# Value pages loaded straight from the cache, and no page copied while index queries run: a hybrid decoder step on one Trainium2 core

## The reference

```python
h = _rmsnorm(x, g_mix_pre)
q, k, v, iq, ik, iw, u = jnp.split(h @ w_in, IN_OFFSETS, axis=-1)
# sample rows: index scores over the paged indexer keys, then attention over the kept keys
ik_past = cache_kidx_l[page_table]
s = relu(einsum('bqhd,bsd->bqsh', iq, ik_all) * IDX_DIM**-0.5)
scores = einsum('bqsh,bqh->bqs', s, iw * N_IDX_HEADS**-0.5)
idx = top_k(scores, 256)
k_sel = cache_k_l[phys, slot]; v_sel = cache_v_l[phys, slot]
a = softmax(q @ k_sel * HEAD_DIM**-0.5) @ v_sel
p = pooling mixer of u (windows 2, 4, 8, 16)
x = x + _rmsnorm([a ; p] @ w_o, g_mix_post)
x = x + _rmsnorm(conv_gated_ffn(_rmsnorm(x, g_ffn_pre)), g_ffn_post)
```

## Time and profile before

| | |
|---|---|
| median of 3 runs | 1183.36 us |
| the profiled execution | 1183.83 us |
| its span, first to last instruction | 1182.0 us |
| mean granted clock | 0.994 |
| PE busy | 1155.7 us, 98% |
| DVE busy | 806.9 us, 68% |
| ACT busy | 531.5 us, 45% |
| POOL busy | 55.3 us, 5% |
| DMA moved | 238.76 MB, mean 202 GB/s |

### The profile page before, as it was taken

The page is one execution under the profiler, slowest core; times in us unless marked ns, Lnnn a source line. Parts: engine busy times, 40 slices in busy tenths (PEclk is TensorE's granted clock), DMA queues, the critical chain, the costliest instruction groups (busy, mean ns, idle before and its releaser), DMA issues.

```text
span 1182.0 us, 25876 instructions
## 1 busy us (share of the span) xinstructions
PE 1155.7 (98%) x9172; PEld 1119.0 (95%) x9172; DVE 806.9 (68%) x1523; ACT 531.5 (45%) x753; POOL 55.3 (5%) x66
## 2 busy tenths in 40 slices
PE   8989999999998999999999999999999999999998
PEld 7879999867897899999999999999999999999997
DVE  4775798876478877777777777777777544444443
ACT  7342333434245655454545454545455433333332
POOL 4710000000003100000000000000000000000000
PEclk9999999999999999999999999999999999999999
DMA  8977878768852565545555555555556866666651
GB/s 310 317 262 246 257 244 304 256 211 274 306 202 91 184 206 164 189 164 188 167 185 169 184 171 181 171 183 170 183 168 185 264 178 179 180 180 185 181 166 74
DMA packets 81080, 238.76 MB, mean 202 GB/s; under 512 B 9440, under 2 KB 28992, under 8 KB 78704
## 3 DMA queue, kind: packets, MB, share of 16 engines
q1 hardware_dynamic: 75152, 225.40, 59.5%
q10 hardware_dynamic: 4480, 9.01, 2.2%
q0 software_dynamic: 1408, 3.84, 1.0%
HBM read 231.64 MB, written 24.16 MB: 216 GB/s over the span
## 4 chain that ended last, share of the span: by engine, by line
PE 89%; DVE 4%; DMA 2%; SPq 2%; issue 1%; ACT 1%; POOL 0%; DVEq 0%; ACTq 0%; POOLq 0%
PE bank L1475 28%; PE bank L1476 28%; PE bank L1478 28%; DMA raw<-in_w_in 2%; DVE part L1344 1%; DMA cache_ring<-kscr 1%; DVE lo L443 1%; PE bank L1692 1%; SPq L486 1%; SPq L485 1%; DVE h_lo L1349 1%; PE bank L1668 0%; PE bank L1844 0%; SPq L484 0%; PE bank L1657 0%
## 5 line engine op out<-in xcount | busy, mean ns | idle before, releaser
L1475 PE MATMUL bank<-h_hi,hi 128*128 128x266 f32 (+1 forms) x2096 | 604.1, 288 | 1.5 <-DVE lo L443 1.5
L1478 PE MATMUL bank<-h_hi,lo 128*128 128x266 f32 (+1 forms) x2096 | 602.8, 288 | 0.0
L1476 PE MATMUL bank<-h_lo,hi 128*128 128x266 f32 (+1 forms) x2096 | 602.1, 287 | 0.0
L443 DVE TENSOR_TENSOR lo<-raw,hi 128x1024 fp32r<-128x1024 f32 (+2 forms) x362 | 431.6, 1198 | 208.1 <-ACT hi L435 194.5
L435 ACT ACTIVATE hi<-raw 128x1024 fp32r<-128x1024 f32 (+2 forms) x362 | 373.5, 1034 | 287.8 <-PE bank L1478 265.0
L1475 PEld LDWEIGHTS bank<-h_hi,hi 128*128 128x128 f32 x2096 | 397.4, 190 | 6.0 <-issue 3.9
L1476 PEld LDWEIGHTS bank<-h_lo,hi 128*128 128x128 f32 x2096 | 396.0, 189 | 0.1
L1478 PEld LDWEIGHTS bank<-h_hi,lo 128*128 128x128 f32 x2096 | 395.7, 189 | 0.0
L1476 PE MATMUL bank<-g_lo,hi 128*128 128x264 f32 x704 | 200.5, 285 | 0.0
L1478 PE MATMUL bank<-g_hi,lo 128*128 128x264 f32 x704 | 199.6, 284 | 0.0
L1475 PE MATMUL bank<-g_hi,hi 128*128 128x264 f32 x704 | 199.4, 283 | 0.0
(11 more groups left out here) (279 smaller groups left out, 612.6 us busy)
## 6 DMA issues: line engine op xcount, KB each, us to landing
raw<-in_w_up SPq DMA_DIRECT2D x176, 512.0 KB, 3.8
raw<-in_w_in SPq DMA_DIRECT2D x56, 512.0 KB, 5.0
raw<-in_w_down SPq DMA_DIRECT2D x64, 448.0 KB, 3.5
raw<-in_w_o SPq DMA_DIRECT2D x32, 512.0 KB, 4.8
raw<-in_w_down SPq DMA_DIRECT2D x32, 512.0 KB, 3.8
kscr<-in_cache_k SPq DMA_DIRECT2D x64, 128.0 KB
vscr<-in_cache_v SPq DMA_DIRECT2D x64, 128.0 KB
mixed<-kscr SPq DMA_DIRECT2D x8, 512.0 KB, 7.2
```

What stands on the lines that cost most here:

```text
L443: ops.tensor_tensor(lo[:, s, 0:width], raw[:, s, 0:width], hi[:, s, 0:width].bitcast(F32), ALU.subtract).then_inc(done, 1)
L1475: mm(out, w_hi, x_hi[:, k, first:], start=(opens and done == 0), stop=False)
L1476: mm(out, w_hi, x_lo[:, k, first:], start=False, stop=False)
L1478: last = mm(out, w_lo, x_hi[:, k, first:], start=False, stop=(closes and done == total))
```

## The change

- Value pages are no longer copied to `vscr`. `load_v` reads 8 page numbers and issues 8 DMAs of 128 KB from the cache straight into the slot; the waits for the slot stay as they were. POOL issues it for sequences 0, 1, 4 and 7, SP for 2, 3, 5 and 6.
- Key pages are still copied (`key_page`), but none while index queries load: SP issues the loads of index tiles 0 to 7 alone, then 4 key pages, then 3 behind each of the 20 projection tiles.
- POOL loads the causal mask only when the last part of x has landed, and begins the gathers of indexer keys once PE is through index tile 0.
- ACT rounds the first index-query chunk after all 16 blocks of h instead of after 13, and issues the loads of `pool_w` and `state_pool` after the sample index scores instead of before the index heads.

```diff
+        def load_v(eng, b):
+            if b < GROUPS:
+                eng.wait_ge(kq_used, 4)
...
+            for g in range(PAGES):
+                n = PAGES * b + g
+                page = eng.value_load(ptrow[0:1, n:n + 1], min_val=0, max_val=a["cache_v"].shape[0] - 1)
+                eng.dma_start(value_slot(b)[:, g, :], a["cache_v"][page]).then_inc(v_loaded[b], 16)
...
-                sp.dma_start(vscr[n], a["cache_v"][page]).then_inc(scr_loaded, 16)
...
+            for t in range(8):
+                load_in(0, C_IQ + 2 * t, t)
             sp.wait_ge(pt_loaded, 48)
...
+            for n in range(4):
+                key_page(n)
+            def paced_in(i, t, n0):
+                load_in(i, C_IQ + 2 * t, 2 * i + t)
+                for k in range(3):
+                    key_page(6 * i + n0 + k)
+            with sp.Fori(0, 10) as i:
+                paced_in(i, 8, 4)
+                paced_in(i, 9, 7)
...
                 if u in (5, 6):
-                    load_v(2 * u - 10)
-                    load_v(2 * u - 9)
-            load_v(4)
+                    load_v(sp, u - 3)
             load_wo(17)
-            load_v(5)
+            load_v(sp, 5)
             load_wo(18)
-            load_v(6)
-            load_v(7)
+            load_v(sp, 6)
...
+            pool.wait_ge(x_loaded[len(X_PARTS) - 2], 16)
             pool.dma_start(S[:, :], a["causal"]).then_inc(s_loaded, 16)
             pool.wait_ge(kix_ready, 1)
+            pool.wait_ge(chunk_used, C_IQ + 2)
...
+            for b in (0, 1, 4, 7):
+                load_v(pool, b)
...
-                if k == 13:
-                    hi_chunk(ae, 0, C_IQ)
                 nc.scalar.activation(h_hi[:, k, :], x0[:, k, :], ACT.Copy,
                                      scale=par[:, G1 + k:G1 + k + 1]).then_inc(h_hi_ready, 1)
+            hi_chunk(ae, 0, C_IQ)
             hi_chunk(ae, 0, C_IQ + 1)
...
-                    pe.wait_ge(v_loaded[GROUPS * r + j], 16)
+                    pe.wait_ge(v_loaded[GROUPS * r + j], 16 * PAGES)
```

More of the change, by code:

```diff
@@ L320, in build_program @@
     kscr = nc.dram_tensor("kscr", [DB * PAGES, P, KV * PAGE], F32).ap()
-    vscr = nc.dram_tensor("vscr", [DB * PAGES, P, KV * HD], F32).ap()
     xscr = nc.dram_tensor("xscr", [P, KM, TG], F32).ap()
@@ L463, in load_x @@
             eng.dma_start(x0[:, part_n, :], a["x"][:, part_n, :]).then_inc(x_loaded[n], 16)
+        def load_v(eng, b):
+            if b < GROUPS:
+                eng.wait_ge(kq_used, 4)
+            elif b == GROUPS:
+                eng.wait_ge(score_done, NU)
+            elif b == GROUPS + 1:
+                eng.wait_ge(pv_done, NU)
+            else:
+                eng.wait_ge(spv_done, 1)
+            for g in range(PAGES):
+                n = PAGES * b + g
+                page = eng.value_load(ptrow[0:1, n:n + 1], min_val=0, max_val=a["cache_v"].shape[0] - 1)
+                eng.dma_start(value_slot(b)[:, g, :], a["cache_v"][page]).then_inc(v_loaded[b], 16)
         @block.sync
@@ L480, in _, with key_page @@
                     load(0, C_IK + j, a["w_ik"][:, j * 8 * IKW:(j + 1) * 8 * IKW], 8 * IKW)
-            def pages(n):
+            def key_page(n):
                 page = sp.value_load(ptrow[0:1, bass.ds(n, 1)], min_val=0, max_val=a["cache_k"].shape[0] - 1)
                 sp.dma_start(kscr[n], a["cache_k"][page]).then_inc(scr_loaded, 16)
-                sp.dma_start(vscr[n], a["cache_v"][page]).then_inc(scr_loaded, 16)
             w_in = a["w_in"]
@@ L493, in load_in @@
                     load(r, cj + j, w_in[t, :, j * CW:(j + 1) * CW])
-            load_in(0, C_IQ, 0)
+            for t in range(8):
+                load_in(0, C_IQ + 2 * t, t)
             sp.wait_ge(pt_loaded, 48)
[L498 to L517, removed]
+            for n in range(4):
[7 more added lines that the diff above has]
+                paced_in(i, 9, 7)
+            k_src = kscr.rearrange("(b g) p e -> b p g e", b=DB)
             def load_k(r, c):
@@ L523, in load_k @@
                     b, pages_c = GROUPS * r + j, key_pages(c)
[L524 to L535, removed]
+                    sp.dma_start(page_slot(b)[:, pages_c], k_src[b][:, pages_c]).then_inc(k_loaded[j][c], 16)
             def load_wo(n):
@@ L543, in _ @@
                 load_wo(n)
-            sp.wait_ge(scr_loaded, 2 * DB * PAGES * 16)
+            sp.wait_ge(scr_loaded, DB * PAGES * 16)
             sp.wait_ge(sidx_done, 1)
@@ L679, in _ @@
             root(1)
-            ae.wait_ge(h_lo_ready, KM)
-            ae.dma_start(partf[:, 0:2048], a["pool_w"]).then_inc(poolw_loaded, 16)
-            ae.dma_start(partf[:, 2048:2048 + 960], a["state_pool"]).then_inc(poolw_loaded, 16)
             IDX_SCALE = float(IDX_DIM) ** -0.5 * float(IDX_HEADS) ** -0.5
@@ L724, in _ @@
                                  scale=IDX_SCALE).then_inc(srelu_done, 1)
+            ae.wait_ge(h_lo_ready, KM)
+            ae.dma_start(partf[:, 0:2048], a["pool_w"]).then_inc(poolw_loaded, 16)
+            ae.dma_start(partf[:, 2048:2048 + 960], a["state_pool"]).then_inc(poolw_loaded, 16)
             with ae.Fori(0, 7) as i:
```

## The result

| | before | after |
|---|---|---|
| median of the runs compared | 1184.24 us (6 runs) | 1190.46 us (6 runs, 1187.93 to 1191.10) |
| ratio after to before | | 1.0041, interval 1.0031 to 1.0051 |
| profiled execution, its span | 1183.83, 1182.0 us | 1190.06, 1188.3 us |
| mean granted clock | 0.994 | 0.990 |
| DMA moved | 238.76 MB | 230.37 MB |

The change made the kernel slower, by about 4.9 us (3.7 to 6.0) as the ratio has it; the forecast was 1186.1 us, 2.7 us above the median of the runs shown then. The two medians of the table lie 6.2 us apart, which is outside that interval; the text goes by the ratio on record. A second comparison (number 6) gave 1.0039 (1.0026 to 1.0052), with medians 4.7 us apart.

A forecast was written before the change was run, and what follows sets the result against it. PE, busy 1155.7 of 1182.0 us, was taken as the bound. From 1183.83 us: start -1.0, index stage -1.6, its clock -1.5, value pages +5.6, clock there +1.0 gave 1186.3, set at 1186.1 us; range 1180 to 1193.5.

The forecast's parts named there:

- second rival: At the value pages, POOL's page read is dear, 1.6 us or more: 1194.5 us; chance 0.13.
- Its own case: At the value pages, POOL decides at 1.2 to 1.5 us a page: 1185.5 to 1190 us; chance 0.36.
- Index stage: At its end, ACT's wait for a late chunk goes and PE resumes sooner: -1.6 us.
- Its clock: Around projection tile 0, matmuls regain full clock: at most 3.1 us, about half entered, -1.5 us.
- Start: Mask leaves the early DMA crowd, ACT's first index chunk moves back: first index matmul 1.0 us earlier, bounds 0.3 and 1.3.
- Moved, priced at nothing: Moved gathers, key pages and ACT's two loads, and half the copying gone, would not change PE's time.
- signs of being wrong: No wait before line 1692, ACT waiting for `raw` in the projections, or PE waiting at line 1606 for the gathers.
- Value pages: Pages issued in series stall PE before the second values: +5.6 us, POOL at 1.35 us a page, SP's 4.3 hidden.
- third rival: Gains of 4 to 5 us equal a value stall of 4 to 5, SP alone deciding: 1183 to 1185 us; chance 0.26.
- first rival: At the value pages, issue cost is small, 1.1 us on SP, 0.9 on POOL, stall 2.0: 1180 us; chance 0.20.
- first values' stall: SP's part there at 294.5 us for first values starting at 294.55: 0 us of stall.
- Clock at the values: Behind the stall at the values the granted clock falls: about 1.5 us lost in a like stretch, +1.0 us entered.

The follow-up runs named there:

- number 6: The changed kernel run once more, unaltered, for a second profile: 1189.88 us.
- Number 4: The kernel before with only direct value pages from the cache; key pages, start and gathers as before: 1190.10 us, ratio 1.0041 to the kernel before.
- number 5: The kernel before with only the two start edits (later mask load, later first index chunk on ACT): 1184.33 us against 1185.20, ratio 0.9992.
- number 8: The changed kernel with a sequence's eight page numbers read ahead of the wait for its slot: 1189.95 us, ratio 1.0043 to the kernel before.
- number 3: The changed kernel with POOL's three late loads moved ahead of its value pages: 1185.90 us, ratio 1.0009 to the kernel before.
- number 9: The changed kernel with all reads early, SP's 32 before its wait for copied keys, POOL's behind the gathers: 1187.68 us against 1185.30, ratio 1.0027.
- number 10: The kernel of number 9 with POOL's three late loads also ahead of its value pages: 1186.87 us, ratio 1.0015 to the kernel before.
- number 12: The changed kernel with SP's reads, eight each, ahead of four w_o loads, POOL's behind the gathers: 1182.44 us against 1184.66, ratio 0.9983.

## Why the prediction came out as it did

Direction and range held (the range ended at 1193.5 us, below the second rival's 1194.5, which it should have held); the forecast of +2.7 us was some 2 us low against the ratios' +4.9 and +4.6. Its own case, that POOL decides at 1.2 to 1.5 us a page, did not come: SP decided. That the size of the stall came out near is luck, since two errors in it cancelled. Step by step:

- **Index stage**, predicted -1.6: -1.5 and -0.3. The reason holds: ACT has no wait for a chunk between 11 us and the end of the stage, and DVE's last index queries start at 78.86. Number 4 shows that it was the value copies.
- **Its clock**, predicted -1.5 of at most 3.1: -1.2 at the end and -0.8 at 44 us in the first profile. In the second, tile 0 began at full clock, as in every later kernel without the wait. There the clock gave 2.7 us (77.77 to 89.52 for what took 80.26 to 96.59 before, less 1.85 us of waits), near the upper bound. The stretch at 44 us took between 8.0 and 9.5 us from one execution to the next whatever the kernel, so that its -0.8 proves nothing.
- **Start**, predicted -1.0: -0.8, and -0.57 in number 5.
- **Moved, priced at nothing**: held for PE, which waits neither at line 1601 for the gathers nor in the projections (busy for all of 84 to 205 us). But one of the signs of being wrong came: ACT waits for `raw` in the projections, 14.4 us in six waits, the longest 5.5, where it was 8.2 us in three before. All six lie between 179 and 201 us, in the last projection tiles; PE stayed busy, so the key pages are closer to too dense than the working had them, and cost nothing yet.
- **Value pages**, predicted +5.6, measured 1.1 + 5.6 = 6.7 (and 7.2 in the second profile). The total hides that the working was wrong in three sizes. POOL takes 1.14 us a page and not 1.35, so it is through at 307.0, not 311.9, and SP decides, not POOL; that was the third rival's picture. SP takes 1.09 us and not 1.2: its last page left at 310.3 instead of 312.1 (the first rival had 310.5). Against these, the landing of SP's last page was mis-sized: 5.36 us where I had 3, since I priced it near the quiet row of 2.1 us and gave no price to POOL's three loads, which the change moved beside SP's last pages. So SP's part was there at 315.6, where the working had 315.1 for it. The sum also let the pages move with PE; in number 6 PE came 3.6 us earlier and they only 1.8. I had also put the first values' stall at nothing: it was 1.1 us in the first profile, where a single issue of SP took 1.56 us instead of 0.33, and none in the second.
- **Clock at the values**, predicted +1.0: +1.3 and +2.6. From the second values to the first sum of squares after them it is 56.6 us without a stall, 56.6 behind one of 1.5 us (number 8), 58.1 behind 3.0 (number 3), 57.9 behind 5.5, 59.4 and 59.2 behind 5.7 and 7.2 (number 4 and the second profile).

The page read was priced at 0.78 us and is 0.56 (number 9); with the DMA a page is 1.1. The floor of 600 ns that the Trainium skill ("DMA: Bandwidth & Descriptors", section "Latency and other measured facts") gives for `tensor_load` is not borne out: it is 0.27 us here, and a page 1.09 or 1.14 us, not the 1.5 estimated by that rule. The fit of a landing on the same page of the Trainium skill (section "Anatomy of one DMA — SWDGE (gpsimd) path"), 2.3 us for a page as an estimate, is for GpSimd's queue. The trace of the change does not agree: POOL's value pages landed in 3.3, 5.6 and 3.8 us (medians by slot).

What stays open: whether POOL's three loads cost anything once no page is waited for (number 10), what decides in one execution that the clock falls at 44 or 232 us, and how much of the loss is that fall, 3.2 us in the first profile.

## What to carry to other kernels

Turning a few large DMAs with fixed addresses into many with looked-up ones cost about 1 us in DMAs here and 7 us in the queue that issues them: count the register reads per page and see what stands beside them. Reads could be taken early for nothing (number 12), but early means in that queue's idle time, ahead of the blocking load before them. Just ahead of their own wait they gained nothing (number 8), and in a block where the queue was needed they delayed another transfer (number 9). And before pricing a landing, list what every other queue issues in the same microseconds.

## What the runs showed of the hardware

- A register read from SBUF with the work on it took 0.56 us on SP (load 0.27, address 0.15, the rest between), and 31 in a row did not overlap at all. A 128 KB DMA took 0.33 us to issue on SP and 0.55 on POOL.
- SP's last 128 KB page landed in 2.06 us, and in 5.24 to 6.07 where another queue had issued three DMAs (976 KB) up to 4.6 us before it.
- The granted clock fell from 2.4 to 1.2 GHz behind each of the waits of 2.7, 3.0, 5.5, 5.7 and 7.2 us at the values, and behind none of those of 0.5, 1.1 and 1.5 us. Behind the wait of 2.55 us at line 1711, before 232 us, it did so in 9 of 11 executions.
